# One predicated copy in place of two masked exponentials per head group, and an accumulating store of y, in a chunked two-way scan

## Chip, cores and metric

The kernel runs on one core of a Trainium2 chip. The metric is the device time of one execution, in microseconds (us). The kernel before has a median of 2822.95 us over three runs (2816.64 to 2823.3).

## What is computed

The reference runs two blocks of a network one after the other, each on 1024 tokens of 1024 features in float32. The change lies in the second block, in its bidirectional state-space scan (SSD). Sixteen heads of 64 values share two groups of B and C rows (128 states). The sequence is cut into 8 chunks of 128 tokens. For a direction, with `acs` the running sum of dt times a within a chunk:

```python
seg = acs[:, :, :, None] - acs[:, :, None, :]
decay = jnp.exp(jnp.where(lower, seg, -jnp.inf))
cb = jnp.einsum('bctgn,bcsgn->bctsg', cc, bc)
y_diag = jnp.einsum('bctsgr,bcsgrp->bctgrp', cb[..., None] * decay, xdt)
st = jnp.einsum('bcsgn,bcsgr,bcsgrp->bcgrpn', bc, jnp.exp(acs[:, :, -1:] - acs), xdt)
...
y_off = jnp.einsum('bctgn,bcgrpn,bctgr->bctgrp', cc, s_in, jnp.exp(acs))
...
return y_f + rev(y_b), s_f, s_b
```

`y_scan + d_skip * xs` goes on to a gate, a norm and an output product. Within a chunk, the forward direction needs the tokens up to the target, the backward one those from the target on. Both contain the target itself.

## The kernel before

The second block is one sequence of stages, each a block of instructions for all engines, with a barrier between stages. `phase4` (L1955) makes the projections, the convolutions and the rows of the scan. `phase5` (L2333) is the scan. `phase6` (L2712) is the gate, the norm and the output product.

**phase4.** TensorE makes 12 tiles of `xbc`, ScalarE takes each out of PSUM (`raw_out`, L2117), VectorE runs a convolution of 5 taps over it (`convolve`, L2262, operations L2267 and L2269), ScalarE applies SiLU, and TensorE transposes the value tiles (`transposes`, L2045) for ScalarE to copy out (L2140). VectorE's order is written out: four B and C tiles (`first_tiles`), then a loop over pairs of value tiles (L2298). At its end VectorE splits the running sums (L2313, L2314), TensorE transposes them (L2099), and VectorE makes `x_rows` and `l_rows` from them (L2327, L2328). It also rounds the identity and two mask squares into `v.square` (L2323, L2324).

**phase5, backward sweep (L2441 to L2450, L2653 to L2665).** It goes over the chunks from the last to the first. Per chunk y is `d_skip` times the values (L2656) plus the carried state's part, and ScalarE's queue stores it to `d.y_tok[c]` in HBM (L2543). The large projections of z and u run beside this on TensorE, so that it is full there.

**phase5, forward sweep (L2480 to L2511).** Per chunk i, in the order of each queue:

- TensorE, `forward(i)`: the carried state's part into PSUM (L2484), then, once y of chunk i-1 has been summed, the chunk's addition to the state (L2490). Then `exponents(i+1)`: four jobs, one for each pair of group g (8 heads) and direction r. A job is two products of the identity with a mask square (L2467, -infinity stand-ins) and two products of `l_rows` with `moving` (L2470, 64 rows), into PSUM pair r. A job waits until the exponential two jobs earlier has read its pair. Then `products_cb(i+1)` (L2476), and the chunk's own part in 16 products of one head each (L2500).
- ScalarE: four exponentials of 128x1024 out of PSUM (L2569), the copy of C·B (L2577, `copy_cb`), `make_moving(i+2)` in 16 operations (L2533, which waits for all jobs of chunk i+1), and in the first five chunks the high part of a pooled tile (L2590, `a_hi`). Then it issues the store of y (L2592).
- VectorE: it adds the two directions' exponentials for each group (L2675), sums y of chunk i-1 (`last_sum`, L2680) and, in five chunks, makes the low part of a pooled tile (L2683, `a_lo`, which waits for L2590). Then it multiplies by C·B into `weights` (L2692, twice), scales the carried state's part (L2699, `fore`), adds it to the y that was loaded back (L2702), brings the state forward (L2705, L2706) and weighs the next values (L2605).
- SyncE: it loads y of the backward sweep back into SBUF (L2405) and the pooled tiles for the split (L2409). Its first y load of each buffer waits for the backward stores, the later ones for the store two chunks earlier.
- GpSimd: nothing, once it has split its last weights.

At the end TensorE makes the first pooled products for `phase6` (L2516), ScalarE waits for its stores of y (L2593, L2594), and the barrier follows. `phase6` loads three pooled tiles (L2748), all of y (L2749) and all of z (L2750) on one queue.

Of the kernel before, what the change touches and what calls it, by code (L numbers as in the profile page):

```python
# [9 lines left out]
F32R = mybir.dt.float32r  # L10
ACT = mybir.ActivationFunctionType
# [1928 lines left out]
def open_scan(nc, ctx, k):  # L1940
# [6 lines left out]
    v.consts, v.square = sb("scan_consts", [P, SCAN_COLS]), sb("scan_square", [P, 3, P], F32R)  # L1947
# [3 lines left out]
    v.rows = sb("head_rows", [P, 80])  # L1951
    return v


def phase4(nc, k, d, v):  # L1955

    with ExitStack() as ctx:
        def sb(n, shape, dt=F32):
# [13 lines left out]
        dt_rows = v.bc[0:32, 3, :]  # L1972
        dt_ctx = regions[0][0:32, TOK2:TOK2 + CTX]
# [6 lines left out]
                                   "evac_ready raw_ready conv silu padded t_done0 t_done1 t_free0 t_free1")  # L1980
# [20 lines left out]
        def _(pe):  # L2001
# [198 lines left out]
        def _(dve):  # L2200
# [122 lines left out]
            dve.tensor_copy(v.square[:, 0, :], k.mats[:, IDENT, :]).then_inc(s["chain"], 1)  # L2323
            dve.tensor_copy(v.square[:, 1:3, :], v.consts[:, 0:2 * P].rearrange("p (r t) -> p r t", r=2)).then_inc(s["chain"], 1)  # L2324
# [4 lines left out]
            ch.n += 4  # L2329
# [3 lines left out]
def phase5(nc, k, d, v):  # L2333
# [4 lines left out]
    with ExitStack() as ctx:  # L2338
# [3 lines left out]
        def over(n, tile):  # L2342
# [21 lines left out]
        weights = [spare[:, 0:SEQ], spare[:, SEQ:2 * SEQ]]  # L2364
# [3 lines left out]
        s = signals(nc, ctx, "p5", "chain xw_ready moving_ready d_done e_ready e_sum w_ready cb_done cb_ready off_done fore_ready fore_added "  # L2368
                                   "st_done state_ready diag_done y_ready y_back y_out0 y_out1 y_in0 y_in1 z_out d_out "
                                   "d_in dhi dlo x_done x_free0 x_free1 cleared area_in pooled")  # L2370
        x_free = [s["x_free0"], s["x_free1"]]
        y_in, y_out = [s["y_in0"], s["y_in1"]], [s["y_out0"], s["y_out1"]]
# [4 lines left out]
        EXPS = 2 * NGRP  # L2377
        ident_r, masks = v.square[:, 0, :], [v.square[:, 1 + r, :] for r in range(2)]
# [16 lines left out]
        def _(sp):  # L2395
            stream_load(sp, k, XBC_END + 4, UZ_END + 4)
            sp.wait_ge(s["z_out"], 16 * KT)
            for i in range(NC):
                if i < 2:
                    sp.wait_ge(s["y_back"], 16 * NC)  # L2400
                else:
                    sp.wait_ge(y_out[i % 2], 16 * (i // 2))
                if i == 1:
                    sp.wait_ge(k.tile_done, UZ_END)
                sp.dma_start(y_of[i % 2], d.y_tok[i, :, :]).then_inc(y_in[i % 2], 16)  # L2405
                if i < SPLIT_EARLY:
                    sp.wait_ge(s["d_out"], 16 * KT)
                    sp.wait_ge(s["dlo"], i)
                    sp.dma_start(stage[:, :], d.u_scr[i, :, :]).then_inc(s["d_in"], 16)  # L2409

        @block.gpsimd
        def _(pool):
            pool.memset(big[:, 0:2, :], 0.0).then_inc(s["cleared"], 1)
            pool.memset(pad[:, :], 0.0).then_inc(s["cleared"], 1)
            stream_split(pool, k, XBC_END + 2, UZ_END + 2)

        @block.tensor
        def _(pe):
# [36 lines left out]
            def exponents(i):  # L2455

                pe.wait_ge(s["moving_ready"], i + 1)
                for j in range(EXPS):
                    g, r, use = j // 2, j % 2, EXPS * i + j
                    if use >= 2:  # L2460
                        pe.wait_ge(s["e_ready"], use - 1)
                    if i and j == 0:
                        pe.wait_ge(s["cb_ready"], i)
                    rows = slice(r * P // 2, (r + 1) * P // 2)
                    outs = [k.ps[:, 2 * r + b, :].rearrange("p (h t) -> p h t", t=P) for b in range(2)]
                    for out in outs:
                        pe.matmul(out, ident_r, bc(masks[r], 1, HPG // 2), start=True, stop=False)  # L2467
                    for b, out in enumerate(outs):
                        at = g * HPG + b * HPG // 2
                        ins = pe.matmul(out, v.l_rows[rows, here(i)], moving[rows, at:at + HPG // 2, :], start=False, stop=True)  # L2470
                    ins.then_inc(s["d_done"], 1)

            def products_cb(i):
                pe.wait_ge(s["e_ready"], EXPS * i + 3)
                for g in range(NGRP):
                    ins = pe.matmul(k.ps[:, 0, g * P:(g + 1) * P], v.bc[:, g, here(i)], v.bc[:, NGRP + g, here(i)],  # L2476
                                    start=True, stop=True)
                ins.then_inc(s["cb_done"], 1)

            def forward(i):  # L2480
# [4 lines left out]
                ins.then_inc(s["off_done"], 1)  # L2485
                pe.wait_ge(s["xw_ready"], back + NC + i + 1)
# [5 lines left out]
                if i + 1 < NC:  # L2492
                    exponents(i + 1)
                    products_cb(i + 1)
                pe.wait_ge(s["fore_ready"], i + 1)
                for h in range(SSM_HEADS):
                    g, cols = h // HPG, slice(h % HPG * P, (h % HPG + 1) * P)
                    if h % HPG == 0:
                        pe.wait_ge(s["w_ready"], 2 * i + g + 1)
# [639 lines left out]
```

## Time and profile before

| | |
|---|---|
| median of 3 runs | 2822.95 us (2816.64 to 2823.3) |
| the profiled execution's own time | 2829.5 us |
| its span | 2827.7 us |
| TensorE busy | 95% |
| VectorE, ScalarE, GpSimd busy | 59%, 22%, 35% |
| mean granted clock of TensorE | 0.976 of full speed |

The profiled execution is one execution. Its span is the time between its first and last instruction, and its own time stands 6.5 us (0.2%) above the median of the runs. Durations below come from it. TensorE's busy share is over the whole kernel. What a change in the forward sweep is worth has to be read from that sweep alone, from 1733 to 1845 us of the span, and from the borders of the stage.

### The profile page before, as it was taken

How to read it: one execution, taken by the hardware profiler on the slowest of the kernel's cores; microseconds unless marked ns; L12 is line 12 of the kernel's file. 1: busy time of each engine (PE TensorE's matmuls, PEld its weight loads, DVE VectorE, ACT ScalarE, POOL GpSimd, SP SyncE). 2: the span in 40 equal slices, each digit the busy share in tenths (PEclk: the TensorE clock that was granted, in tenths of full speed). 3: DMA queues.
4: the chain of work that ended last, by engine and by line, in shares of the span. 5: the costliest groups of instructions: out<-in, count | busy, mean ns of one | idle time of the engine just before them, and what ended most of it. 6: DMA issues, size and time to landing. Idle time of an engine off the chain costs nothing. (4 is left out here: it accounts for less than half of the span.)

```text
span 2827.7 us, 32173 instructions
## 1 busy us (share of the span) xinstructions
PE 2672.9 (95%) x12390; PEld 2146.4 (76%) x12390; DVE 1658.7 (59%) x2219; ACT 608.1 (22%) x871; POOL 988.0 (35%) x515
## 2 busy tenths in 40 slices
PE   8889999999999999987888999989989999999997
PEld 5778777778888888866775776578767888888885
DVE  6887555756556665676747986953475222222247
ACT  4222242311110011133232104632131110001111
POOL 2122225554333343541212432012645333333353
PEclk9999999999999999998999999999989999999998
DMA  3111132223222332221001343241322111111122
GB/s 139 39 51 45 51 142 82 97 82 98 97 89 91 102 96 96 97 101 61 31 30 38 112 127 112 99 177 45 116 93 90 53 45 47 50 52 45 52 69 102
DMA packets 88484, 228.88 MB, mean 81 GB/s; under 512 B 27520, under 2 KB 30720, under 8 KB 88384
## 3 DMA queue, kind: packets, MB, share of 16 engines
q1 hardware_dynamic: 52384, 172.81, 18.3%
q10 hardware_dynamic: 36000, 54.69, 6.1%
q8 instruction: 68, 1.11, 0.2%
q14 instruction: 32, 0.26, 0.0%
HBM read 197.98 MB, written 28.31 MB: 80 GB/s over the span
## 5 line engine op out<-in xcount | busy, mean ns | idle before, releaser
L215 POOL CAST w_hi<-w_raw 128x1024 fp32r<-128x1024 f32 x254 | 289.0, 1138 | 1774.6 <-PE ps L228 1755.8
L224 PE MATMUL ps<-a_hi,w_hi 128*128 128x512 f32 x2080 | 694.7, 402 | 47.3 <-PEq L2942 14.5
L217 POOL TENSOR_TENSOR w_lo<-w_raw,w_hi 128x1024 fp32r<-128x1024 f32 x254 | 696.0, 2740 | 20.3
L226 PE MATMUL ps<-a_lo,w_hi 128*128 128x512 f32 x2080 | 677.9, 393 | 0.0
L228 PE MATMUL ps<-a_hi,w_lo 128*128 128x512 f32 x2080 | 676.7, 393 | 0.0
L224 PEld LDWEIGHTS ps<-a_hi,w_hi 128*128 128x128 f32 x2080 | 391.4, 191 | 151.0 <-issue 58.3
L226 PEld LDWEIGHTS ps<-a_lo,w_hi 128*128 128x128 f32 x2080 | 396.1, 190 | 83.3
L228 PEld LDWEIGHTS ps<-a_hi,w_lo 128*128 128x128 f32 x2080 | 395.3, 190 | 84.3
L226 PE MATMUL ps<-g_b,w_hi 128*128 128x512 f32 x1216 | 412.6, 391 | 0.0
L224 PE MATMUL ps<-g_b,w_hi 128*128 128x512 f32 x1088 | 364.4, 392 | 11.2 <-DVE g_b L1806 11.2
L228 PE MATMUL ps<-g_b,w_lo 128*128 128x512 f32 x1088 | 362.1, 390 | 0.0
L226 PEld LDWEIGHTS ps<-g_b,w_hi 128*128 128x128 f32 x1216 | 229.6, 189 | 47.1
L224 PEld LDWEIGHTS ps<-g_b,w_hi 128*128 128x128 f32 x1088 | 204.8, 188 | 62.1 <-DVE g_b L1806 15.0
L228 PEld LDWEIGHTS ps<-g_b,w_lo 128*128 128x128 f32 x1088 | 204.8, 188 | 42.9
L1886 DVE TENSOR_TENSOR tmp_b<-tmp_b 128x1024 f32<-128x1024 f32 x48 | 58.8, 1225 | 298.8 <-ACT tmp_b L1764 298.8
L1764 ACT ACTIVATE tmp_b<-ps 128x1024 f32<-128x1024 f32 x48 | 49.4, 1029 | 849.1 <-PE ps L228 849.1
L1899 DVE TENSOR_TENSOR mix_b<-mix_b,ps 128x1024 f32<-128x1024 f32 x48 | 58.5, 1220 | 235.2 <-PE ps L228 235.2
L1888 DVE TENSOR_TENSOR g_b<-tmp_b,g_b 128x1024 fp32r<-128x1024 f32 x48 | 106.4, 2217 | 54.2 <-ACT g_b L1768 54.2
L1158 DVE TENSOR_TENSOR acc_b<-acc_b,tmp_b 128x512 f32<-128x512 f32 x56 | 77.0, 1375 | 23.3 <-ACT tmp_b L1117 19.7
L2269 DVE SCALAR_TENSOR_TENSOR cv<-raw,vecs,cv 128x1284 f32<-128x1284 f32 (+1 forms) x48 | 80.4, 1676 | 5.3 <-DVE cv L2267 0.6
L1878 DVE SCALAR_TENSOR_TENSOR ada_sum_b<-ada_w,c_silu,ada_sum_b 128x128 f32<-128x128 f32 x252 | 74.6, 344 | 3.0
L1878 DVE SCALAR_TENSOR_TENSOR ada_sum_b<-ada_w_b,c_silu,ada_sum_b 128x128 f32<-128x128 f32 x252 | 74.6, 343 | 3.0
(459 smaller groups left out, 2682.2 us busy)
## 6 DMA issues: line engine op xcount, KB each, us to landing
w_raw<-in_wstream SPq DMA_DIRECT2D x254, 512.0 KB, 3.5
ada_w<-in_ada_w ACTq DMA_DIRECT2D x25, 512.0 KB, 3.5
ada_w_b<-in_ada_w ACTq DMA_DIRECT2D x25, 512.0 KB, 3.5
y_by_token<-y ACTq DMA_DIRECT2D x12, 512.0 KB, 3.3
x_res_b<-in_xT SPq DMA_DIRECT2D x2, 2048.0 KB, 11.2
x_block<-x_res_b SPq DMA_DIRECT2D x16, 256.0 KB, 3.0
z_rows<-ada_w ACTq DMA_DIRECT2D x8, 512.0 KB, 2.9
u_rows<-pad ACTq DMA_DIRECT2D x8, 512.0 KB, 4.2
```

The lines of the kernel that those rows point to most:

```text
L215: pool.tensor_copy(k.w_hi[:, s, :], k.w_raw[:, s, :]).then_inc(k.w_high, 1)
L217: pool.tensor_tensor(k.w_lo[:, s, :], k.w_raw[:, s, :], k.w_hi[:, s, :].bitcast(F32), ALU.subtract).then_inc(k.w_split, 1)
L224: pe.matmul(o, w_hi, a_hi[:, c], start=first, stop=False)
L226: pe.matmul(o, w_hi, a_lo[:, c], start=False, stop=False)
L228: ins = pe.matmul(o, w_lo, a_hi[:, c], start=False, stop=last)
L1158: dve.tensor_tensor(w.acc[:, cols], w.acc[:, cols], w.tmp[:, t % 2, cols], ALU.add).then_inc(self.added, 1)
L1764: act.activation(w.tmp[:, t % 2, :], pair[t % 2], ACT.Relu).then_inc(k.pair_free[t % 2], 1)
L1878: ins = dve.scalar_tensor_tensor(out=sums, in0=weights, scalar=k.c_silu[:, kt, c:c + 1], in1=sums, op0=ALU.mult, op1=ALU.add)
L1886: tt(w.tmp[:, t % 2, :], w.tmp[:, t % 2, :], w.tmp[:, t % 2, :], ALU.mult).then_inc(s["square"], 1)
L1888: tt(w.g_lo[:, t, :], w.tmp[:, t % 2, :], w.g_hi[:, t, :].bitcast(F32), ALU.subtract)\
L1899: tt(w.mix[:, 2 * t, :], w.mix[:, 2 * t, :], pair[q], ALU.add).then_inc(k.pair_free[q], 1)
L2269: ins = stt(out=out, in0=raw[:, m:m + cols], scalar=tap(m), in1=out, op0=ALU.mult, op1=ALU.add)
```

## The change

In `phase5`, the two directions' exponents of a head group are both made by TensorE without masks, one in each PSUM pair, by four products of 64 rows (128x512 each). VectorE then copies the backward exponents over the forward ones where the source token comes after the target (`copy_predicated`, with the mask of L3071 as predicate). ScalarE takes one exponential of that. The diagonal then counts once, so the backward direction's own term, dt times the sum over states of C times B, is made in `phase4` and joins `d_skip` as a weight per token and head (`v.own`), which the backward sweep uses in L2656. The forward sweep no longer loads y back: y is the sum of two terms, and a transfer issued by GpSimd adds it to `d.y_tok`. The weights are made in place in `big`, which now alternates between two halves.

```diff
 (phase4, TensorE, before the transposes of the sums)
+            pe.wait_ge(k.pair_free[1], XBC_END // 2)
+            pe.wait_ge(s["own_in"], len(own_bc[0]) + len(own_bc[1]))
+            for g in range(NGRP):
+                for c0, c1, home in own_bc[g]:
+                    for c in range(c0, c1):
+                        ins = pe.matmul(own_sums[:, g * NC + c:g * NC + c + 1], home[:, (c - c0) * P:(c - c0 + 1) * P],
+                                        k.mean_col[:, :], start=True, stop=True)
+            ins.then_inc(s["own_out"], 1)
             pe.wait_ge(s["sums_ready"], 1)
-            pe.wait_ge(k.pair_free[1], XBC_END // 2)
 (phase4, VectorE, between the tiles of B and C and the loop over value tiles)
             first_tiles(3)
+            dve.wait_ge(s["silu"], 2 * XS0)
+            for g in range(NGRP):
+                for c0, c1, home in own_bc[g]:
+                    tt(home, v.bc[:, g, c0 * P:c1 * P], v.bc[:, NGRP + g, c0 * P:c1 * P], ALU.mult).then_inc(s["own_in"], 1)
 (phase4, VectorE, at the end)
-            dve.tensor_copy(v.square[:, 0, :], k.mats[:, IDENT, :]).then_inc(s["chain"], 1)
-            dve.tensor_copy(v.square[:, 1:3, :], v.consts[:, 0:2 * P].rearrange("p (r t) -> p r t", r=2)).then_inc(s["chain"], 1)
+            dve.wait_ge(s["own_out"], 1)
+            for g in range(NGRP):
...
+                ch.link(tt(v.own[:, :, hs], dt[:, 0:NC, rear], bc(own_sums[:, g * NC:(g + 1) * NC], 2, HPG), ALU.mult))
+            ch.link(stt(out=v.own[:, :, :], in0=v.own[:, :, :], scalar=1.0 * D_MODEL,
+                        in1=bc(v.rows[:, 64:64 + SSM_HEADS], 1, NC), op0=ALU.mult, op1=ALU.add))
 (phase5, SyncE)
             sp.wait_ge(s["z_out"], 16 * KT)
-            for i in range(NC):
...
-                sp.dma_start(y_of[i % 2], d.y_tok[i, :, :]).then_inc(y_in[i % 2], 16)
...
+            sp.wait_ge(s["d_out"], 16 * KT)
+            for i in range(SPLIT_EARLY):
+                sp.wait_ge(s["dlo"], i)
+                sp.dma_start(stage[:, :], d.u_scr[i, :, :]).then_inc(s["d_in"], 16)
 (phase5, GpSimd)
             stream_split(pool, k, XBC_END + 2, UZ_END + 2)
+            pool.wait_ge(s["y_back"], 16 * NC)
+            for i in range(NC):
+                pool.wait_ge(s["y_ready"], NC + i + 1)
+                pool.dma_start(d.y_tok[i, :, :], y_of[i % 2], accum_op=ALU.add).then_inc(y_out[i % 2], 16)
+            for q in range(2):
+                pool.wait_ge(y_out[q], 16 * NC // 2)
 (phase5, TensorE)
+            def exponents(i, g):
                 pe.wait_ge(s["moving_ready"], i + 1)
+                if i or g:
+                    pe.wait_ge(s["e_ready"], NGRP * i + g)
+                if i and g == 0:
+                    pe.wait_ge(s["cb_ready"], i)
+                for b in range(2):
+                    at = g * HPG + b * HPG // 2
+                    for r in range(2):
+                        rows = slice(r * P // 2, (r + 1) * P // 2)
+                        ins = pe.matmul(k.ps[:, 2 * r + b, :].rearrange("p (h t) -> p h t", t=P), v.l_rows[rows, here(i)],
+                                        moving[rows, at:at + HPG // 2, :], start=True, stop=True)
+                ins.then_inc(s["d_done"], 1)
 (phase5, order in forward(i) now:
  L2484, exponents(i+1, 0), L2490, exponents(i+1, 1), wait for fore, own_chunk(i, 0), products_cb(i+1), own_chunk(i, 1);
  products_cb waits for both choices and writes bank 2)
 (phase5, ScalarE)
             def exps(i):
-                for j in range(EXPS):
...
+                if i >= 2:
+                    act.wait_ge(s["diag_done"], i - 1)
...
+                for g in range(NGRP):
+                    act.wait_ge(s["chosen"], NGRP * i + g + 1)
+                    act.activation(big[:, i % 2 * NGRP + g, :], pair[0], ACT.Exp).then_inc(s["e_ready"], 1)
...
-                act.wait_ge(s["y_ready"], NC + i + 1)
-                act.dma_start(d.y_tok[i, :, :], y_of[i % 2]).then_inc(y_out[i % 2], 16)
 (phase5, VectorE)
-                ch.link(tt(heads(y_even[:, :]), values(c), bc(v.rows[:, 64:64 + SSM_HEADS], 2, HDIM), ALU.mult))
+                ch.link(tt(heads(y_even[:, :]), values(c), bc(v.own[:, c, :], 2, HDIM), ALU.mult))
...
+            def choose(i, g):
+                dve.wait_ge(s["d_done"], NGRP * i + g + 1)
+                fore, rear = (p.rearrange("p (h t) -> p h t", h=HPG) for p in pair)
+                dve.copy_predicated(fore, bc(after, 1, HPG), rear).then_inc(s["chosen"], 1)
...
-                dve.wait_ge(s["fore_added"], i + 1)
-                tt(y_of[i % 2], y_of[i % 2], Xf[(i + 1) % 2], ALU.add).then_inc(s["y_ready"], 1)
+                if i >= 2:
+                    dve.wait_ge(y_out[i % 2], 16 * (i // 2))
...
+                tt(y_of[i % 2], fore_tmp, Xf[(i + 1) % 2], ALU.add).then_inc(s["y_ready"], 1)
 (phase5, VectorE, order in chunk i now:
  the two weights (wait for C·B i and each exponential), last_sum(i-1) with a_lo, fore(i), choose(i+1, 0),
  state times decay, choose(i+1, 1), state plus addition, weigh(i+1))
```

## Rows read from the trace of the kernel before

**Rows 1.** Busy time by stage: length, PE, PEld, DVE, ACT, POOL, clock, DMA.
```profile
1733.00:1845.00 112.00, 104.98 (x485) 63.66 (x486) 97.40 (x84) 73.81 (x159) 2.75 (x2) 1.00 0.29 104
```
**Rows 2.** VectorE's timeline, forward sweep: the sums of y (start us, us).
```profile
1754.41 1.22 DVE L2680 TENSOR_TENSOR y<-y,ps 128x1024 f32<-128x1024 f32 x1 [1.88 <-PE ps L2500]
...
1822.97 1.21 DVE L2680 TENSOR_TENSOR y_odd<-y_odd,ps 128x1024 f32<-128x1024 f32 x1
...
1835.58 1.22 DVE L2680 TENSOR_TENSOR y<-y,ps 128x1024 f32<-128x1024 f32 x1 [0.87 <-PE ps L2500]
...
1844.08 1.22 DVE L2680 TENSOR_TENSOR y_odd<-y_odd,ps 128x1024 f32<-128x1024 f32 x1 [0.16 <-PE ps L2500]
```
**Rows 3.** VectorE's timeline, one chunk: additions, low part, y from before.
```profile
1766.58 2.35 DVE L2675 TENSOR_TENSOR big<-big 128x1024 f32<-128x1024 f32 x2
...
1770.40 1.22 DVE L2683 TENSOR_TENSOR a_lo<-ada_w,a_hi 128x1024 fp32r<-128x1024 f32 x1 [0.34 <-ACT a_hi L2590]
...
1775.14 1.23 DVE L2702 TENSOR_TENSOR y<-y,pad 128x1024 f32<-128x1024 f32 x1
```
**Rows 4.** TensorE's timeline, the same chunk.
```profile
1770.21 1.96 PE L2490 MATMUL ps<-xw,tok 128*128 128x512 f32 x4 [0.84 <-DVE y_odd L2680]
...
1773.23 0.73 PE L2467 MATMUL ps<-scan_square 128*128 128x512 f32 x2
1773.89 0.73 PE L2470 MATMUL ps<-moving,l_rows 64*128 64x512 f32 x2
...
1777.19 0.71 PE L2476 MATMUL ps<-bcT 128*128 128x128 f32 x4
1777.74 3.68 PE L2500 MATMUL ps<-tok 128*128 128x64 f32 x32
```
**Rows 5.** ScalarE's timeline, the same chunk.
```profile
1777.30 1.02 ACT L2569 ACTIVATE big<-ps 128x1024 f32<-128x1024 f32 x1 [0.30 <-PE ps L2470]
1778.22 0.38 ACT L2577 ACTIVATE pad<-ps 128x256 f32<-128x256 f32 x1
1778.49 4.77 ACT L2533 ACTIVATE moving<-x_rows,scan_consts 128x128 fp32r<-128x128 f32 x16
1783.16 1.04 ACT L2590 ACTIVATE a_hi<-ada_w 128x1024 fp32r<-128x1024 f32 x1
```
**Rows 6.** Waits in the forward sweep: total us, times, longest.
```profile
ACT big L2569 <- PE ps L2470: 17.9, 26, 3.9
...
DVE a_lo L2683 <- ACT a_hi L2590: 4.1, 5, 1.6
```
**Rows 7.** Chain of work, a gemm of phase6: two full products of 512 columns.
```profile
1898.00 0.45 PE ps L226 x2
```
**Rows 8.** VectorE's timeline, an operation of one input from PSUM with two scalars.
```profile
1521.56 1.34 DVE L2327 TENSOR_SCALAR x_rows<-ps,scan_consts 128x1024 f32<-128x1024 f32 x1 [1.73 <-PE ps L2099]
```
**Rows 9.** Timelines in phase4: the places where the new work goes.
```profile
1390.15 1.15 ACT L2151 ACTIVATE bcT<-cv 128x512 f32<-128x512 f32 x2 [6.26 <-DVE cv L2269]
...
1392.93 0.95 DVE L2267 TENSOR_SCALAR cv<-raw,vecs 128x1284 f32<-128x1284 f32 x1 [2.81 <-ACT raw L2125]
...
1419.93 1.45 PE L2045 MATMUL ps<-mats,cv 128*128 128x128 f32 x5 [4.68 <-ACT tok L2140]
...
1519.55 1.97 PE L2099 MATMUL ps<-mats,sums 128*128 128x128 f32 x8 [2.98 <-DVE sums L2314]
```
**Rows 10.** DMA issues: KB each, median us from issue to landing.
```profile
y<-y_by_token SPq DMA_DIRECT2D x4, 512.0 KB, 3.8
y_by_token<-y_odd ACTq DMA_DIRECT2D x4, 512.0 KB, 2.6
```
**Rows 11.** Timeline and chain at the border of phase5 and phase6.
```profile
1848.98 0.61 PE L228 MATMUL ps<-a_hi,w_lo 128*128 128x512 f32 x2
...
1851.00 0.70 PE L224 MATMUL ps<-a_hi,w_hi 128*128 128x512 f32 x2 [1.41 <-PEq L2942]
...
1852.75 25.76 DMA mix_b<-z_rows
```

More of the change, by code:

```diff
@@ L10 @@
 F32R = mybir.dt.float32r
+I32 = mybir.dt.int32
 ACT = mybir.ActivationFunctionType
@@ L1951, in open_scan @@
     v.rows = sb("head_rows", [P, 80])
+    v.own = sb("own_weight", [P, NC, SSM_HEADS])
     return v
@@ L2376, in phase5 @@
         BWD_JOBS = 2
-        EXPS = 2 * NGRP
-        ident_r, masks = v.square[:, 0, :], [v.square[:, 1 + r, :] for r in range(2)]
+        after = v.consts[:, SC_FORE:SC_FORE + P].bitcast(I32)
         back = 2 * CC
@@ L2453, in here @@
                 return slice(i * P, (i + 1) * P)
-            def exponents(i):
+            def exponents(i, g):
                 pe.wait_ge(s["moving_ready"], i + 1)
-                for j in range(EXPS):
[L2459 to L2471, printed above, removed]
+                if i or g:
[9 more added lines that the diff above has]
+                ins.then_inc(s["d_done"], 1)
@@ L2473, in products_cb, with own_chunk @@
             def products_cb(i):
-                pe.wait_ge(s["e_ready"], EXPS * i + 3)
+                pe.wait_ge(s["chosen"], NGRP * (i + 1))
                 for g in range(NGRP):
-                    ins = pe.matmul(k.ps[:, 0, g * P:(g + 1) * P], v.bc[:, g, here(i)], v.bc[:, NGRP + g, here(i)],
+                    ins = pe.matmul(k.ps[:, 2, g * P:(g + 1) * P], v.bc[:, g, here(i)], v.bc[:, NGRP + g, here(i)],
                                     start=True, stop=True)
                 ins.then_inc(s["cb_done"], 1)
+            def own_chunk(i, g):
+                pe.wait_ge(s["w_ready"], NGRP * i + g + 1)
+                for h in range(g * HPG, (g + 1) * HPG):
+                    cols = slice(h % HPG * P, (h % HPG + 1) * P)
+                    ins = pe.matmul(Xf[(i + 1) % 2][:, h * HDIM:(h + 1) * HDIM], big[:, i % 2 * NGRP + g, cols],
+                                    v.tok[:, i, VAL + h * HDIM:VAL + (h + 1) * HDIM], start=True, stop=True)
+                return ins
@@ L2485, in forward @@
                 ins.then_inc(s["off_done"], 1)
+                if i + 1 < NC:
+                    exponents(i + 1, 0)
                 pe.wait_ge(s["xw_ready"], back + NC + i + 1)
@@ L2492, in forward @@
                 if i + 1 < NC:
-                    exponents(i + 1)
+                    exponents(i + 1, 1)
+                pe.wait_ge(s["fore_ready"], i + 1)
+                own_chunk(i, 0)
+                if i + 1 < NC:
                     products_cb(i + 1)
[L2495 to L2499, printed above, removed]
-                    ins = pe.matmul(Xf[y_at][:, h * HDIM:(h + 1) * HDIM], weights[g][:, cols],
-                                    v.tok[:, i, VAL + h * HDIM:VAL + (h + 1) * HDIM], start=True, stop=True)
-                ins.then_inc(s["diag_done"], 1)
+                own_chunk(i, 1).then_inc(s["diag_done"], 1)
             for q in range(2):
                 pe.wait_ge(k.pair_free[q], UZ_END // 2)
-            exponents(0)
+            for g in range(NGRP):
+                exponents(0, g)
             products_cb(0)
```

78 lines of the change are left out of this document (34 added, 44 removed).

## The prediction

> **What bounds the kernel now.** TensorE is the bound of the kernel as a whole, but the change sits almost wholly in the forward sweep, so I read that stretch by itself. The busy times by stage show it as 112 us in which TensorE works 105 and VectorE 97 [rows 1]: both are near full, and halving one engine's work need not shorten the stage. VectorE's timeline gives the period. The eight sums of y start at 1754.41, then five periods take 68.56 us (13.71 each), one takes 12.61 and the last 8.50 [rows 2]. From the sweep's start at 1733.36 to the first sum it is 21.05 us, and to the end of the last one 111.9.
>
> The timelines of one chunk say what fills a period. VectorE runs eleven operations of 1.22 us that start 1.13 to 1.3 us apart [rows 3]. TensorE hardly pauses: four jobs of exponents at 1.32 us each (a mask pair and an exponent pair, 0.66 us apiece), C·B, then the 32 passes of the own part at 0.115 us each [rows 4]. ScalarE's `make_moving` alone is 4.77 us, and `a_hi` stands behind it [rows 5]. The wait table names the coupling: ScalarE waits for exponents 26 times, and VectorE's `a_lo` waits for `a_hi` in all five chunks that have one, 4.1 us in total [rows 6]. So the sweep is bound by queues that hand work to each other, and that handing over is what I follow.
>
> **Engine work saved in the sweep.** Per chunk VectorE loses two additions of exponentials and the addition of the loaded y, three operations of 1.22 us [rows 3], and gains two choices. TensorE loses eight mask products and keeps eight of 64 rows. ScalarE loses two exponentials of 1.02 [rows 5] and the store's issue. SyncE loses eight y loads, nothing of which was waited for. None of that is a gain by itself. It is one only if nothing else sets the period.
>
> **The new round trip.** PSUM pair 0 and pair 1 are both taken by one group, so group 1's products wait for group 0's exponential, which waits for its choice. I price the steps from start to start, with 0.08 us for a hop between engines:
> - the products of one group. No row shows four 64-row products that alternate between partitions 0 to 63 and 64 to 127. Upper end: they run at the pace of the row, 0.33 each, 1.32 with 0.11 to finish [rows 4]. Lower end: the two halves run side by side and each pair costs what a full product costs in a gemm, 0.225 [rows 7], 0.45 for the four. I take the nearest row's pace, 0.33 a product [rows 4], with the halves side by side: 0.66, plus 0.14 to finish and a hop, 0.88.
> - the choice. An operation with one PSUM input takes 1.22 [rows 2]; one out of PSUM with scalars 1.34 [rows 8]. I take 1.22, plus a hop 1.30, and keep 1.34 for the range. The upper end, if the instruction also read its destination, is twice the row, about 2.3.
> - the exponential and a hop: 1.11 [rows 5].
>
> With `a_lo` in the chunk the circle is: `a_lo` to `fore` 1.14, to the first choice 1.14, to the exponential 1.30, to the second products 1.11, to the second choice 0.88. Then TensorE still does half of the own part (1.83) before C·B (0.71): 2.40 from the second choice to `copy_cb`. Then 0.27 to `make_moving`, 4.67 to `a_hi`, 1.08 to `a_lo` [rows 4, 5]. Sum **13.99 us**, against 13.71: VectorE's ten operations fit into 11.7, but it would wait 2 us for `a_hi`. Without `a_lo` the circle runs from `make_moving` (4.85 with the hop) to the products 0.88, 1.30, 1.11, 0.88, 2.40, 0.27: **11.69**, against 12.61. The last chunk has no exponents behind it: y sum 1.30, state products 1.73, own part 3.91, **6.94** against 8.50. The start: products 0.88, choice 1.30, exponential 1.11, products 0.88 with a first hop make 4.25, exponential and copy 2.5, `make_moving` 4.85, one more round 4.16, five VectorE steps at 1.14: 21.46, against 21.05.
>
> Sweep: +0.4, five times +0.28 = +1.4, -0.9, -1.6: **-0.7 us**.
>
> The Trainium skill, page "TensorE: Matmul & The Clock Gate", section Part 3 on packing small matmuls, says that products whose operands start in different row groups run concurrently. By that rule and the gemm's pace the four products would cost 0.45, 0.2 less than I take; a circle holds them twice, and the sweep would come to -2.8 us. No row here shows two halves side by side, and my sum does not need the rule.
>
> **phase4.** VectorE's five products over 2048 columns need the last SiLU of tile 3, done at 1391.30 [rows 9]. They run 1.14 for 1024 columns and 1.4 for the rest (384, 256, 256 and 128, from 1.22 per 1024 with the fixed part) and end near 1394.0. The next convolution started at 1392.93 after 2.81 us of idle [rows 9], so it slips 1.1. That convolution feeds SiLU, transposes and ScalarE's copies, for which TensorE already idles 4.68 at 1419.93 [rows 9]: the slip reaches TensorE, **+1.1**. TensorE's sixteen products of one column take 32 passes at 0.115 [rows 4], 3.7 us, in the 2.98 that it idled before the transposes of the sums [rows 9]: **+0.7**. The three small VectorE operations that wait for them, about 0.9 in a chain, hide behind the transposes (1.97), and two copies go. Both ends: 0, if a step there is hidden after all, and +4.
>
> **The end of the stage.** Before, the last sum ended at 1845.30 [rows 2], its store landed 2.6 after its issue [rows 10], and TensorE finished later, at 1849.6; phase6 began 1.4 after that [rows 11]. Now GpSimd adds the last y into HBM. The trace shows no accumulating transfer. Lower end: as fast as the store, hidden, 0. Upper end: a read and a write in turn, 3.8 + 2.6 = 6.4 [rows 10], and some 1 us of GpSimd before it (a guess: no row shows a transfer of its queue). Its landing is then 1.3 + 0.1 + 1 + 6.4 = 8.8 after the last sum's start, against TensorE's 5.5: +3.3. I take 5.6 for the transfer, since adding needs the read first: **+2.5**. Nothing covers it: phase6 starts with the loads of y and z, and z's 25.76 us are on the chain that ended last [rows 11]. Inside the sweep the same transfer is covered: `last_sum(i)` waits for the one two chunks earlier, 27 us before.
>
> The backward sweep reads another weight of the same shape: nothing. The pooled tiles' loads on SyncE lose the y loads ahead of them and keep their wait for `a_lo`: nothing.
>
> **Sum.** -0.7 + 1.1 + 0.7 + 2.5 = **+3.6 us** on the profiled execution's 2829.5, so 2833.1. It stands 0.2% above the median of the runs. On the median 2822.95 it is **2826.6**.
>
> **The rivals.**
> - *The halves do not overlap* (22%). The round trip then holds 1.32 twice. For it: the row's pairs go at 0.33 a product though a gemm's go at 0.225 [rows 4, 7], so these products already run below pace. Against: those pairs use the same half of the array. Each period grows to 14.65 and 12.98, the start to 23.98: the sweep +6.4, in all +10.7, **2833.7**, slower. It decides from about 1.1 us per group on.
> - *VectorE becomes the bound* (12%). If `a_hi` and the round trip keep out of the way, a period is 10 operations at 1.17, 11.7 [rows 3]: five times -2.0, then -1.2 and -1.6, with +4.3 around it -8.5: **2814.5**. Against: `make_moving` and `a_hi` are unchanged and already late [rows 6].
> - *The accumulating transfer is slow* (10%). At 11 us to land, the border costs 5 more, **2832**; over 26 us it would stop `last_sum` too.
> - *The choice costs two passes* (6%), 2.3 instead of 1.22. Two of them in each circle: +16, **2843**.
>
> My forecast has the remaining 50%. That the edit does nothing is excluded by its counts: 16 exponentials for 32.
>
> **Chances.** A measurement of this kernel can tell about 0.3% from no change, 8.5 us. Slower: most of the first rival, part of the third, the fourth: 0.28. Faster: part of the second: 0.10. The range goes from the side-by-side halves with a free border and half of the VectorE case, 2817, to the first rival with a choice of 1.34 and the full border, 2837.
>
> **What would show it.** In the profile after: L2470's successor in 0.66 us steps or 1.32; the choice at 1.22; `a_lo` waiting some 2 us for `a_hi`; y sums 14.0 apart, later 11.7; GpSimd's transfers landing near 5.6 us and TensorE idle some 4 us at the border; TensorE's gap near 1420 at 5.8. Periods below 13 in the first five chunks would make the circle wrong.

## The result, and the profile after

The changed kernel takes 2841.69 us (median of seven runs), against 2822.95 us before: a ratio of 1.0066, with a 95% interval of 1.0046 to 1.0086. It is slower, by twice what a measurement can tell, and it lies above the range. One of its seven runs (6807.59 us) and one of the twelve of e11 below (12990.03 us) were in a slow state, and no ratio counts them. The profiled execution took 2841.68 us, with a span of 2839.8 us.

The span is longer by 12.1 us. I cut it at places that both traces have. From the first context sum of `phase4` to the first weighing of `phase5` it is 217.2 us for 214.2: **+3.0**. The sweep, from its first product to the start of its last sum of y, is 120.5 for 110.7: **+9.8**. From there to the issue of the load of z it is 10.4 for 8.7: **+1.8**. That is 14.6; the other stretches together are 2.5 shorter. Their code is the same but for the weight that the backward sweep reads, and 2.5 us is within the spread of one kernel's own runs (2816.64 to 2827.72 us for the kernel before).

So the sweep is what went wrong. Here it is by window, from one sum of y to the next (length, busy PE, PEld, DVE, ACT, POOL, granted clock, DMA share, GB/s). Before, the clock stood at 1.00 over the whole of it [rows 1].

```profile
1735.95:1759.92 23.97, 17.09 (x68) 9.18 (x68) 14.07 (x12) 13.68 (x34) 2.37 (x2) 0.79 0.18 66
1759.92:1776.24 16.32, 11.65 (x50) 9.28 (x50) 11.68 (x11) 8.10 (x22) 1.02 (x1) 0.74 0.29 65
1776.24:1791.85 15.61, 13.47 (x53) 9.65 (x53) 11.69 (x10) 8.05 (x21) 0.87 (x1) 0.72 0.31 67
1791.85:1805.85 14.00, 12.59 (x56) 6.88 (x55) 11.53 (x11) 8.06 (x21) 0.86 (x1) 0.88 0.33 75
1805.85:1820.43 14.58, 11.19 (x50) 8.02 (x50) 11.59 (x11) 8.03 (x21) 0.89 (x1) 0.72 0.32 74
1820.43:1835.90 15.47, 13.41 (x53) 9.50 (x53) 11.69 (x11) 8.05 (x21) 0.88 (x1) 0.72 0.22 34
1835.90:1849.55 13.65, 12.68 (x56) 6.98 (x55) 10.38 (x9) 4.17 (x9) 0.86 (x1) 0.87 0.26 40
1849.55:1856.42 6.87, 5.67 (x38) 4.58 (x38) 4.79 (x6) 0.00 (x0) 0.86 (x1) 1.00 0.49 76
```

Read the length together with the clock: it is below 1.00 in every window but the last. VectorE works 87.4 us in the eight windows together, 9.1 less than over the same stretch of the kernel before, so it isn't what got longer:

```profile
1733.36:1844.08 110.72, 104.06 (x481) 62.90 (x482) 96.48 (x83) 73.55 (x158) 2.39 (x2) 1.00 0.29 105
```

TensorE's timeline in the second window shows what the clock does to it:

```profile
1762.44 1.99 PE L2515 MATMUL ps<-xw,tok 128*128 128x512 f32 x4
1767.46 0.88 PE L2484 MATMUL ps<-moving,l_rows 64*128 64x512 f32 x4 [3.04 <-ACT big L2590]
1768.27 3.67 PE L2499 MATMUL ps<-tok,big 128*128 128x64 f32 x16
1771.73 1.17 PE L2491 MATMUL ps<-bcT 128*128 128x128 f32 x4
1772.69 3.51 PE L2499 MATMUL ps<-tok,big 128*128 128x64 f32 x16
```

It waits 3.04 us for the exponential (L2590). After that, 16 passes of the own part take 3.5 to 3.7 us, where 32 took 3.68 before [rows 4]. That is half speed, the 1.2 GHz level of the clock. Two views of the stretch from 1733 to 1860 follow. The first is the group of the choices (count, busy us, mean ns, idle before), the second is waits (total us, times, longest):

```profile
L2692 DVE COPY_PREDICATED ps<-scan_consts,ps 128x1024 f32<-128x1024 int32 x16 | 19.6, 1225 | 15.6 <-PE ps L2484 15.6
```
```profile
ACT big L2590 <- DVE ps L2692: 43.8, 15, 4.2
PE ps L2484 <- ACT big L2590: 15.2, 7, 3.8
DVE a_lo L2705 <- ACT a_hi L2611: 7.6, 5, 1.6
```

The choice costs what was expected of it, 1.225 us. The wait table shows the round trip: ScalarE waits 15 times for a choice, and TensorE seven times for an exponential. `a_lo` waits 7.6 us for `a_hi`, for 4.1 before [rows 6].

The border, in the DMA table (KB, median us to landing) and in the timeline [rows 10, 11]:

```profile
y_by_token<-y_odd POOLq DMA_DIRECT2D x4, 512.0 KB, 5.3
```
```profile
1861.31 0.61 PE L229 MATMUL ps<-a_hi,w_lo 128*128 128x512 f32 x2
...
1865.11 0.70 PE L225 MATMUL ps<-a_hi,w_hi 128*128 128x512 f32 x2 [3.19 <-PEq L2966]
```

The last transfer is issued at 1858.14, the median one takes 5.3 us, and TensorE idles 3.19 at the border for 1.41 before. And `phase4`, at the places of [rows 9]:

```profile
1384.42 5.25 DVE L2282 SCALAR_TENSOR_TENSOR cv<-raw,vecs,cv 128x1024 f32<-128x1024 f32 x4
...
1393.38 0.94 DVE L2280 TENSOR_SCALAR cv<-raw,vecs 128x1284 f32<-128x1284 f32 x1
...
1420.17 3.15 PE L2051 MATMUL ps<-mats,cv 128*128 128x128 f32 x12 [5.43 <-ACT tok L2153]
1422.97 1.20 PE L225 MATMUL ps<-a_hi,w_hi 128*128 128x512 f32 x2
1423.97 1.05 PE L227 MATMUL ps<-a_lo,w_hi 128*128 128x512 f32 x2
...
1521.20 0.42 DVE L2331 TENSOR_TENSOR sums<-bcT,sums 128x256 fp32r<-128x256 f32 x1
...
1522.04 1.88 PE L2112 MATMUL ps<-mats,sums 128*128 128x128 f32 x8
```

Two rows of the kernel before go with them:

```profile
1384.87 5.25 DVE L2269 SCALAR_TENSOR_TENSOR cv<-raw,vecs,cv 128x1024 f32<-128x1024 f32 x4
...
1519.07 0.42 DVE L2314 TENSOR_TENSOR sums<-bcT,sums 128x256 fp32r<-128x256 f32 x1
```

The two executions reach this stage 0.5 us apart, so distances count here and not times of day. The next convolution starts 8.96 us behind the start of the one before it, for 8.06 before: it slips 0.90. The pause before 1420 is 0.75 longer (4.68 before), and the clock is slow behind it: a gemm pair takes 1.05 instead of 0.6. Over 1420 to 1427 it was granted 0.53, and 0.76 before. The transposes of the sums start 0.42 us behind the end of the split that they wait for, and 0.06 before: the sixteen products stand ahead of them.

### The profile page after: what moved, and what is told of

The parts are those of the page before. It is cut to its first block and busy times, and to the rows that moved or that the text cites. A ratio compares the mean times of both kernels' runs of the same rounds, so it can differ in the third digit from the quotient of the medians.

```text
span 2839.8 us, 32057 instructions
## 1 busy us (share of the span) xinstructions
PE 2672.2 (94%) x12358; PEld 2153.7 (76%) x12358; DVE 1650.6 (58%) x2217; ACT 592.7 (21%) x855; POOL 996.9 (35%) x523
```

## The experiments

The theory: TensorE lost so much work in the sweep that its granted clock no longer stays up, and products at half speed lie on the circle of waits. The rivals: the circle itself is longer than I counted, the accumulating transfer does harm, or the own part does.

**Each part alone.** e3 is the kernel before with the accumulating transfer, e4 the changed kernel without the own part (that term is missing from its output), e7 the changed kernel with the old path of y.

```diff
 (e3, on the kernel before; e7 is the reverse, on the changed one)
-                dve.wait_ge(s["fore_added"], i + 1)
-                tt(y_of[i % 2], y_of[i % 2], Xf[(i + 1) % 2], ALU.add).then_inc(s["y_ready"], 1)
...
+                tt(y_of[i % 2], fore_tmp, Xf[(i + 1) % 2], ALU.add).then_inc(s["y_ready"], 1)
...
 (GpSimd)
+                pool.dma_start(d.y_tok[i, :, :], y_of[i % 2], accum_op=ALU.add).then_inc(y_out[i % 2], 16)
```

> The kernel before, with the accumulating transfer alone: no y loads, no addition of the loaded y on VectorE, the store replaced by GpSimd's adding transfer. TensorE's order is unchanged and it is nearly full, so the clock stays at 1.0. Expected: the border of the stages 1.8 us longer as in the changed kernel (the last transfer lands 5.4 us after its issue), the chunk's period 0 to 0.7 us shorter since TensorE's 12.9 us of work per chunk is next: in all between -4 and +2 us against before (ratio 0.9985 to 1.001). A rival, that the transfer itself costs the sweep: periods longer than 13.7 and more than +5 us.

Measured: 2824.55 us, ratio 0.9994 (0.9984 to 1.0004). Five periods are 13.22 us (13.71 before) at a clock of 1.00, and the border is 10.6 us for 8.7. The last period is an exception to the forecast: 9.83 us for 8.50, at a clock of 0.85. The sweep is 1.0 us shorter in all (109.7 for 110.7), the border takes more than that back, and the time doesn't move.

> The changed kernel without the work in phase4 for the backward direction's own term (five VectorE products, sixteen TensorE products, three small operations); the output lacks that term. Scan stage starts about 2.5 to 3 us earlier than in the changed kernel if that work is what phase4 costs (0.7 of it through TensorE's pause near 1420 us and the lower clock after it, 2.5 through the sixteen products): about -3 us against the changed kernel. If those products were hidden as such work usually is, 0.

Measured: 2840.44 us, ratio 1.005 (1.0037 to 1.0063). `phase4` takes 213.8 us, 3.4 less than in the changed kernel, but the sweep took 122.4, 1.9 more, at a clock of 0.79. The stage's cost is confirmed. In time it is 15.9 us above its own runs of the kernel before, for the changed kernel's 18.7: the 3 us of the forecast would look like that, but the two intervals overlap.

> The changed kernel with the path of y of the kernel before (loads on SyncE's queue, one more sum on VectorE, stores on ScalarE's queue). Theory: the choice with its thin TensorE carries the loss, since adding by transfer alone cost nothing (e3): the clock falls in the sweep again, the last y sum comes 119 to 122 us behind the first exponent product, the border is about 1.8 us shorter, and the time is 2838 to 2842 us. Rival (the accumulating transfer is harmful only together with the choice, by the wait of the y sum for a buffer): 2826 us or below.

Measured: 2837.63 us, ratio 1.0045 (1.0031 to 1.006). First exponent product to last y sum is 118.6 us, at a clock of 0.81, and the border is 8.7 us again. Time and sweep are both just under the forecast. The choice with its thin TensorE carries the loss: of the 9.8 us that the sweep lost, 7.9 are there without the transfer. The 1.9 us between the two sweeps are no more than what e4's sweep is away from the changed kernel's with the same code.

**Less work for TensorE, and nothing else.** This is the test that decides between the clock and the choice: the kernel before without its mask products. (The exponentials are taken with scale 0, so the output has no decays.) There is no choice in it, no transfer, no own part.

```diff
-                    for out in outs:
-                        pe.matmul(out, ident_r, bc(masks[r], 1, HPG // 2), start=True, stop=False)
...
-                        ins = pe.matmul(out, v.l_rows[rows, here(i)], moving[rows, at:at + HPG // 2, :], start=False, stop=True)
+                        ins = pe.matmul(out, v.l_rows[rows, here(i)], moving[rows, at:at + HPG // 2, :], start=True, stop=True)
...
-                    act.activation(big[:, j, :], pair[r], ACT.Exp).then_inc(s["e_ready"], 1)
+                    act.activation(big[:, j, :], pair[r], ACT.Exp, scale=0.0).then_inc(s["e_ready"], 1)
```

> The kernel before without its eight mask products a chunk; the exponentials are taken with scale 0, so the decays of the output are left out, and all else is in place: no choice, no accumulating transfer, no own part. TensorE has 5.3 us less to do in each chunk. Theory (the clock falls with TensorE's missing work alone): the granted clock of the sweep falls below 0.95 in several periods, state and own products double to 3.8 and 7 us there, and the sweep is no shorter than before's 110.1 us or even longer, although a quarter of TensorE's work is gone; the time is 2820 to 2835 us. Rival (the choice's waits of 3 us or more are needed for it): the clock stays at 1.00 and the sweep shrinks by up to 8 x 0.5 us towards VectorE's own sum, time 2816 to 2824 us.

Measured: **2836.11 us, ratio 1.0033 (1.002 to 1.0045), slower than the kernel before, with eight products less in each chunk.** Its sweep is 120.8 us, 10.1 more than before (110.7; the forecast has 110.1), at a mean clock of 0.77. The views of e6, one of its windows and TensorE's timeline:

```profile
1784.48:1800.34 15.86, 13.55 (x53) 10.06 (x53) 12.84 (x12) 12.25 (x29) 0.00 (x0) 0.74 0.29 100
```
```profile
1790.52 0.73 PE L2468 MATMUL ps<-moving,l_rows 64*128 64x512 f32 x2 [1.92 <-ACT big L2567]
...
1792.36 1.23 PE L2474 MATMUL ps<-bcT 128*128 128x128 f32 x4 [0.20 <-ACT big L2567]
1793.37 6.93 PE L2498 MATMUL ps<-tok 128*128 128x64 f32 x32
```

The own part takes 6.93 us instead of 3.68, and no pause of the stretch is longer than 1.98 us. The time is 1 us above what I had given for it; the mechanism is there without any choice. The rival of e6 is refuted.

**The work put back.** If the clock is the cause, products whose results nobody needs must make the kernel faster. e1 issues the state products (the chunk's addition to the state, L2490 before) twice in each chunk, the same values into the same place, and fills the start; e2 also takes `a_hi` before `make_moving`.

```diff
-                for g in range(NGRP):
+                for g in list(range(NGRP)) * 2:
                     ins = pe.matmul(X[st_at][:, g, :], v.tok[:, i, g * P:(g + 1) * P], xw[:, half_of(g)], start=True, stop=True)
```

> The changed kernel, with TensorE's pause before the second group's products filled: the state products of each chunk are issued twice (1.7 us more work, same result), and once more in the start. Clock theory: the changed kernel lost about 8 of its 10 us in the sweep to TensorE at its lower clock (granted 0.72 to 0.83 in the sweep's chunks), so with more work for TensorE the granted clock goes back to near 1.0, the y sums stand about 14.0 us apart in the first five chunks and 11.7 in the next, the sweep takes 112 us instead of 120, and the run is about 8 us faster than the changed kernel (ratio to before about 1.003). Hand-over theory (the round trip between TensorE, VectorE and ScalarE alone makes the periods of 14 to 16.3): periods stay at 14 to 16.3 or grow by the added 1.7, no gain, whatever the clock.

> e1_filled, with ScalarE's a_hi ahead of make_moving. If the circle through make_moving, a_hi and a_lo sets the period of the first five chunks, as the prediction had it, a_lo no longer waits and the period falls from about 14.0 to about 12.6 (the circle through make_moving alone, 11.7, plus a_hi's 0.93): some 7 us less than e1_filled. If the low clock set the period and a_lo's wait was slack, no change against e1_filled.

Measured: e1 2837.36 us, ratio 1.0044 (1.0031 to 1.0057), mean clock of the sweep 0.90; e2 2839.22 us, ratio 1.0047 (1.0034 to 1.006), clock 0.93. The clock rose as forecast, but both forecasts of the length were missed: the sweeps are 119.6 us, for 112, and 119.7, for some 7 less than e1's. Where the clock was 1.00, e1's period was 13.98 us, but a wait for `moving` was left at the start:

```profile
1751.24 1.22 PE L2484 MATMUL ps<-moving,l_rows 64*128 64x512 f32 x4 [3.56 <-ACT moving L2558]
1752.39 5.91 PE L2515 MATMUL ps<-xw,tok 128*128 128x512 f32 x8
```

Behind 3.56 us of idle the eight state products took 5.91 us instead of 3.70. e2's periods at full clock were 13.55 us, not the 12.6 expected: the doubled products stand ahead of the second exponents, and the choice then waited 2.0 us for those. So e5 keeps e1's products (state products twice in chunks 0 to 5 only) and puts more into the waits themselves: `fill` writes a bank that nobody reads before it is written again.

```diff
+            def fill(n):
+                for _ in range(n):
+                    pe.matmul(k.ps[:, 3, :], v.bc[:, 0, 0:P], v.bc[:, 1, 0:4 * P], start=True, stop=True)
...
                 if i + 1 < NC:
+                    fill(1 if i else 4)
                     exponents(i + 1, 0)
...
                 if i + 1 < NC:
+                    pe.wait_ge(s["chosen"], NGRP * (i + 1) + 1)
+                    fill(1)
                     exponents(i + 1, 1)
```

> The changed kernel with repeated products (same result) in the waits of TensorE: state products twice in chunks 0 to 5, four more products before exponents(1), one before each exponents(i+1, 0) and exponents(i+1, 1). Theory (the clock): if the waits of 3 to 4 us are what lets the granted clock fall, it now stays at 1.00 in all eight periods; the first y sum comes at about 24 us behind the first exponent product (26.1 with e1), five periods are near 14.0 us, the two last near 11.7 and 6.9, so first exponent product to last y sum is about 113 us against 120.5 of the changed kernel, and the time about 2834 us. Rival (the choice on VectorE is the cost whatever the clock): periods stay at 15 us or more although the clock is 1.00, and the time stays at 2837 us or above.

Measured: 2829.19 us, ratio 1.002 (1.0009 to 1.0032). The windows of e5:

```profile
1733.88:1758.13 24.25, 22.62 (x91) 12.01 (x92) 13.98 (x12) 13.63 (x34) 2.38 (x2) 1.00 0.17 65
1758.13:1772.12 13.99, 13.01 (x62) 7.44 (x61) 11.52 (x11) 8.05 (x21) 1.02 (x1) 1.00 0.35 76
...
1828.05:1839.80 11.75, 10.97 (x57) 6.53 (x55) 10.48 (x11) 4.17 (x9) 0.86 (x1) 1.00 0.29 45
1839.80:1846.67 6.87, 5.66 (x38) 4.59 (x38) 4.79 (x6) 0.00 (x0) 0.86 (x1) 1.00 0.49 79
```

The clock is 1.00 in all eight. **Five periods of 13.98 to 13.99 us, then 11.75 and 6.87: the prediction's circle had 13.99, 11.69 and 6.94.** That is no chance meeting of sums: in the second window each of its steps, from `a_lo` to `fore` and on to the next `a_lo`, is within 0.06 us of the step in the prediction. The circle was right and the clock was wrong. The sweep is 112.8 us, as forecast and 7.7 less than in the changed kernel, with more products in it. The time is 5 us below the forecast of 2834; between the two kernels' profiled executions, what the sweep doesn't explain lies in stretches with the same code.

The start of e5 pays for its own products. Its second choice of chunk 1 waits behind the doubled state products and a fill:

```profile
1746.46 0.74 PE L2484 MATMUL ps<-moving,l_rows 64*128 64x512 f32 x4
1747.13 3.70 PE L2520 MATMUL ps<-xw,tok 128*128 128x512 f32 x8
1750.66 1.02 PE L2505 MATMUL ps<-bcT 128*128 128x512 f32 x2
```

That choice starts at 1752.46, 6.00 us behind the products of the first group. In e9 below, with the state products once, it is 4.28 us.

**`phase4`.** e8 keeps VectorE's products of the own part and leaves the sixteen of TensorE out (the term is missing from the output).

> The changed kernel with the three products of the own part on VectorE in stage 4 kept and the sixteen products on TensorE and the ops on own_weight left out (so that term is missing from the output). From the context sums to the first weighing of stage 5 it took 214.2 us before, 217.2 after, 213.8 without the whole own part. Theory: the sixteen products and their ops lie on the path to the last transposes with about 2.3 us, so this run shows about 214.9 us. Rival (the products on VectorE, which push the convolution and stretch a pause of TensorE, are the cost): 216.5 us or more.

Measured in one run: 2842.97 us, and 216.7 us for the stage. The rival has it: the sixteen products and what follows cost some 0.5, which fits the 0.36 us by which the transposes of the sums came later in the changed kernel. The five products on VectorE cost most of the rest (e4, without both: 213.8). e7, with the same code as the changed kernel here, needs a caution: it took 215.8 us. Its pause was as long (5.38), but the clock was up again sooner, 0.91 over 1420 to 1427:

```profile
1418.15 3.15 PE L2051 MATMUL ps<-mats,cv 128*128 128x128 f32 x12 [5.38 <-ACT tok L2153]
1420.96 0.84 PE L225 MATMUL ps<-a_hi,w_hi 128*128 128x512 f32 x2
1421.63 0.62 PE L227 MATMUL ps<-a_lo,w_hi 128*128 128x512 f32 x2
```

So differences below some 1.4 us in this stage can be the clock alone; the 0.5 of e8 by itself is one of them.

**Towards a better version.** e9 has e5's fills, the state products once, and `a_hi` ahead of `make_moving`. e10 adds two moves, e11 fills twice where e10 fills once, and e12 is e10 without any fill.

```diff
 (e9: ScalarE)
                     copy_cb(i + 1)
-                    if i + 2 < NC:
-                        make_moving(i + 2)
                 if i < SPLIT_EARLY:
...
                     act.activation(v.a_hi[:, i, :], stage[:, :], ACT.Copy).then_inc(s["dhi"], 1)
+                if i + 2 < NC:
+                    make_moving(i + 2)
 (e10: phase4, VectorE)
-            first_tiles(3)
-            dve.wait_ge(s["silu"], 2 * XS0)
             for g in range(NGRP):
+                if g:
+                    first_tiles(3)
+                dve.wait_ge(s["silu"], 2 * (XS0 - 1 + g))
 (e10: ScalarE, ahead of the first choice)
+                if i == 0:
+                    act.activation(big[:, 0, 0:1], v.consts[:, 0:1], ACT.Exp, scale=0.0).then_inc(s["table"], 1)
+                    act.wait_ge(s["table"], 1)
 (e11)
-                    fill(1 if i else 4)
+                    fill(2 if i else 4)
```

> As e5 (repeated products in the waits of TensorE), but the state products once only, and ScalarE takes a_hi before moving, so that the low half on VectorE doesn't wait. Same result. Theory (the clock and a circle of waits, both seen in e5): with the clock at 1.00 the periods of chunks 0 to 5 shrink from 13.99 to about 12.6 us, where VectorE's eleven operations bind, the sweep from first exponent product to last y sum is about 105 us (112.8 in e5, 110.1 before), and the time is about 2821 to 2823 us, at or just under the kernel before. Rival (with one pass of state products TensorE is again too thin): the clock falls below 0.95 in some periods, which are then 14 to 16 us, and the time is 2830 us or more.

> e9, with the first half of the own part's products on VectorE taken before the convolution of the fourth tile, where VectorE has waited 1.8 us, and with ScalarE's exponential table loaded before the first choice ends. Same result. Theory (the late products on VectorE are what stage 4 pays for): context sums to first weighing falls from 217 to about 215 us, the start of the sweep is 1.3 us shorter, and the time is 2 to 3 us below e9's. Rival (stage 4 pays for the sixteen products of TensorE at its end): still 216.7 us or more, and only the 1.3 us are gained.

Measured: e9 2826.83 us, ratio 1.0 (0.9989 to 1.0012); e10 2823.69 us, ratio 1.0002 (0.9989 to 1.0015). e9's sweep is 108.0 us, not 105, and its time 4 us above its forecast. e10's `phase4` takes 215.4 us for e9's 217.2, as the theory of the late products said: TensorE's pause near 1420 is 4.76 us again, for 5.59 in e9, and e11 and e12, with the same code there, have 4.68 and 215.6. The start of the sweep was to be 1.3 us shorter and is 0.25 (22.29 for 22.54): the exponential now follows the first choice at once, but the next products still have the start's doubled state products ahead of them. Both sweeps alternate, e10:

```profile
1757.57:1770.25 12.68, 10.96 (x58) 6.72 (x57) 11.51 (x11) 8.04 (x22) 1.02 (x1) 1.00 0.38 84
1770.25:1784.63 14.38, 12.66 (x58) 7.32 (x57) 11.52 (x11) 8.05 (x22) 0.87 (x1) 0.88 0.33 73
```
```profile
1772.98 0.74 PE L2485 MATMUL ps<-moving,l_rows 64*128 64x512 f32 x4 [1.72 <-ACT moving L2566]
1773.65 3.45 PE L2521 MATMUL ps<-xw,tok 128*128 128x512 f32 x4
```

The pause of 1.72 us stands in both kinds of period. In every second one the state products behind it take 3.45 us instead of 1.98.

> e10 with two repeated products instead of one before exponents(i+1, 0) in chunks 1 to 6, where TensorE of e10 still waits 1.72 us for moving. Same result. In e10 the periods are 12.68 us at a clock of 1.00, but every second one is 14.38 us at a clock near 0.86. Theory (the clock): with the wait filled all six are 12.68 us, so the sweep is some 5 us shorter than e10's 107.7 us, and the time is 2818 to 2821 us, below the kernel before. Rival (the 14.38 us have another cause, or the extra products get in the way): the alternation stays or all periods grow to 13.5 us, and the time stays at 2823.7 us or above.

> e10 with all repeated products taken out, so that only the order differs from the changed kernel (a_hi ahead of moving, the first half of the own part early, the table loaded early). Same result. Theory (the clock decides, the order only together with it): TensorE waits through the sweep again, the granted clock falls to 0.7 to 0.9 in its periods, they are 14 to 16 us, the sweep from first exponent product to last y sum is 117 us or more, and the time is 2834 to 2838 us, 10 us or more above e11. Rival (the order alone brought e9's and e10's gain): the sweep is near 107 us and the time near 2823 us.

Measured: e11 2823.57 us beside 2826.57 of the kernel before, ratio **0.9989 (0.9977 to 1.0001)**; e12 2828.58 us, ratio 1.0012 (0.9998 to 1.0026). First e11, then e12:

```profile
1758.45:1771.14 12.69, 11.82 (x60) 7.11 (x59) 11.51 (x11) 8.05 (x22) 1.02 (x1) 1.00 0.37 84
1771.14:1821.90 50.76, 47.28 (x234) 28.43 (x233) 46.06 (x41) 32.21 (x84) 3.50 (x4) 1.00 0.35 73
```
```profile
1760.41:1772.98 12.57, 9.37 (x53) 6.00 (x52) 11.52 (x11) 8.11 (x22) 1.02 (x1) 1.00 0.39 85
1772.98:1787.59 14.61, 12.03 (x53) 7.00 (x52) 11.52 (x12) 7.93 (x21) 0.87 (x1) 0.77 0.30 72
```

With the pause cut to 0.87 us e11 has its five periods of 12.68 to 12.70 us, as forecast, and a sweep of 104.4 us, 6.3 less than before. `phase4` (+1.4) and the border (+1.8) take half of it back. The sweep is 3.3 us shorter than e10's, for a forecast of 5, and the time is above the forecast of 2818 to 2821. Its median is 0.1% below the kernel before and its interval reaches no change, so no gain is shown.

e12 missed its forecast: its sweep is 109.6 us, not 117, and it is only 5 us behind e11, not 10. Its rival (107 us and 2823) is nearer in the sweep, and the time lies between the two. The clock did fall in every second period, but the order alone (`a_hi` first, the table early) took 10.9 us off the changed kernel's sweep (109.6 for 120.5). That is more than the 7.7 that e5's fills took off, and its time can't be told from the kernel before. On top of the order the fills are worth 5.2 us of sweep (104.4 for 109.6).

VectorE's timeline of e11 shows what its 12.69 us are:

```profile
1761.95 1.23 DVE L2706 COPY_PREDICATED ps<-scan_consts,ps 128x1024 f32<-128x1024 int32 x1
...
1765.46 1.23 DVE L2706 COPY_PREDICATED ps<-scan_consts,ps 128x1024 f32<-128x1024 int32 x1 [1.16 <-PE ps L2485]
```

The round trip from the first choice to the second is 3.51 us, one VectorE operation fits into it, and VectorE idles 1.16 us in it. The other eight steps follow each other without a pause.

## Why the prediction was wrong

- **The step that failed is the sweep's -0.7 us.** It took every TensorE duration from rows at a clock of 1.00 [rows 1, 4] for a kernel that gives TensorE eight products less and adds waits. Measured: +9.8. With the clock held up (e5) it was +2.1, so at least 7.7 us are the clock. None of my rivals had it, so the range had no room for it. The signs stood in my own text: TensorE 105 of 112 us busy, "TensorE hardly pauses". That was what the mask products paid for.
- A second term of the same sum was missing: the start. It was 21.46, and e5 has 24.25. Of these 2.8 us, 1.1 are the load of ScalarE's table, 1.28 us behind the first choice, which I had left out; e9, which loads it at the same place, starts in 22.54. The other 1.7 are e5's own products in the start (6.00 us for 4.28). Without them e5's sweep would be some 111.1 us, an estimate from these rows. By that estimate the clock costs the changed kernel 9.4 us of its 120.5, and the rest of the sum was off by 1.1.
- In the same circle the terms held: products 0.66 (0.73 with the end), choice 1.22 (1.225), periods 13.99, 11.69 and 6.94 (13.99, 11.75 and 6.87 in e5). The rivals of halves that don't overlap and of a choice in two passes were wrong. The rival in which VectorE binds never came true as written, at 11.7 us: with `a_hi` out of the way (e11) VectorE still waits 1.16 us in each round trip, and the period is 12.69. The -2.8 us beside the sum counts the products of a group twice in a circle; the circle with `a_lo` holds them once.
- `phase4`: +1.8 predicted, +3.0 measured. The convolution slipped 0.90 for the 1.1 predicted, and TensorE's pause grew by 0.75. The slow clock behind that pause, no term of mine, cost up to 1.4 more (e7). The sixteen products cost 0.4 to 0.5, for the 0.7 predicted.
- The border: +2.5 predicted, +1.8 measured. The transfer lands in 5.3 to 5.4 us for 5.6, and GpSimd issues it in 0.88, for my guess of 1. The rival of a slow transfer was wrong.

The Trainium skill, page "TensorE: Matmul & The Clock Gate", section Part 1, says that the gate holds TensorE at 1.2 GHz by default and that only activity releases it. The runs agree: e6 lost work, and the granted clock of its sweep was 0.77 for 1.00 before. Its table "Why this matters for your kernels" warns of single long gaps between bursts; here the clock also fell where no pause was longer than 1.73 us (e10) or 1.98 us (e6). The rule of its Part 3, with the pace of a gemm, gave an estimate of 0.45 us for the four 64-row products; the rows show 0.66.

What stays open is what in the pattern of work and pauses decides the clock. Neither the length of one pause nor the busy share of a period tells it here. The kernel before keeps its clock behind a pause of 1.97 us, and e2 keeps it in three periods in a row that hold a pause of 2.58 us and have TensorE busy 10.96 of 13.55 us (81%). e10 loses it behind 1.72 us, right after a period in which TensorE was busy 10.96 of 12.68 (86%). The rows of the kernel before and of e2:

```profile
1744.85 0.73 PE L2467 MATMUL ps<-scan_square 128*128 128x512 f32 x2 [1.97 <-ACT moving L2533]
```
```profile
1808.68:1822.23 13.55, 10.97 (x57) 6.73 (x56) 11.52 (x11) 8.05 (x22) 0.89 (x1) 1.00 0.35 78
```
```profile
1811.42 0.73 PE L2484 MATMUL ps<-moving,l_rows 64*128 64x512 f32 x4 [2.58 <-ACT moving L2558]
```

## What to carry to other kernels

Before taking work from TensorE, ask what will keep its clock up. A duration read at full clock need not hold once the engine has less to do than in that row, so price the products on the critical circle at both levels and make the slow one a rival. Where an edit thins TensorE out, look at the granted clock window by window first: a stage that got longer while every engine works less is the sign. Products that nobody needs, placed inside its waits, are a cheap test of that and can be a remedy, but they can also delay the work behind them (e2, the start of e5). Shorten the circle first: here moving two operations on ScalarE's queue took more off the sweep than the fills did.

## What the runs showed of the hardware

- Eight mask products fewer in each chunk made the kernel 0.33% slower (e6): the granted clock of its sweep's windows, 1.00 before, was 0.72 to 0.86 in all but the last.
- Filling TensorE's waits with repeated products brought the changed kernel from 18.7 us above its runs of the kernel before to 5.2 us above (e5). In the profiled executions the sweep has 7.7 us of that.
- A longer pause doesn't always cost the clock more: e2 kept 1.00 with a pause of 2.58 us in each of three periods, and e10 fell to 0.88 in every second period with pauses of 1.72 us.
- A load of ScalarE's table took 1.28 us. Moved ahead of the first choice, it let the exponential start 1.32 us behind the start of the choice, for 2.61 (e10, e9).
- A predicated copy of 128x1024 within PSUM costs 1.225 us, as much as an addition of that size. Four 64-row products on alternating halves issue in 0.66 us, which is what two of them on one half took before [rows 4].
